# Two transformer blocks on one Trainium2 core: reordering block two's query and key chunks, moving v's range to other banks, and one selection product for the compressed blocks

## The chip, the cores and the metric

One core of one Trainium2 chip runs the whole program in one launch. The metric is device time in microseconds for one execution, the median of several. The engines are named as the profile names them: PE is TensorE (matrix products, with PEld its weight loads), DVE is VectorE, ACT is ScalarE, POOL is GpSimd, and SP is SyncE, which here only issues transfers. Each engine runs its own instruction list in order and waits for the others on semaphores.

## The reference, cut to what is computed

Two blocks are applied one after the other to a sequence of 256 tokens of width 1024. The change lies in the second block, in the projection and the attention that follow its first norm:

```python
p = _split_columns(u @ w_in)          # q_a k_a v_a | q_b k_b v_b | q_idx k_idx w_idx | q_c k_cmp v_cmp k_sel v_sel k_win v_win g_c | g_merge
o_a = _stick_breaking(heads(q_a), heads(k_a), heads(v_a))
o_b = _dsa_attention(_rope(q_b), rope1(k_b), v_b, _rope(q_idx), rope1(k_idx), w_idx)
o_c = _nsa_attention(_rope(q_c), rope1(k_cmp), v_cmp, rope1(k_sel), v_sel, rope1(k_win), v_win, gates, ...)
g = sigmoid(g_merge)
merged = g0 * (o_a @ w_up[0]) + g1 * (o_b @ w_up[1]) + g2 * (o_c @ w_up[2])

def _compress(tok, pos_emb, w1, w2):  # inside _nsa_attention, for k_cmp and v_cmp: 15 blocks of 32 tokens
    blocks = tok[:, idx] + pos_emb
    hid = gelu(blocks.reshape(B, n_cmp, 32 * 64) @ w1)   # 128 wide
    return hid @ w2
```

The queries are 4 heads of 64, so each of q_b, q_idx and q_c is 256 columns of the projection; k_b, k_idx, k_sel, k_win, k_cmp and v_cmp are 64 columns each. All inputs and outputs are 32-bit floats.

## The kernel before

**Products in parts.** A large product is computed from split operands. A weight slot arrives by DMA (`low`), ACT rounds it into a high part (`split` in `scalar_program`, by halves of its eight row tiles), DVE subtracts to get the low part (`split` in `vector_program`, L2705), and PE multiplies high by high, low by high and high by low. The high parts stand in two buffers that alternate, so the split of slot j+1 can begin when slot j-1 has been multiplied.

**Block two's projection, `main_b`.** After the two chunks of the `head` (q_a and k_a, in `plan_2[0]` and `plan_2[1]`), a stream `st2` of slots j = 0, 1, 2 ... is worked off. Slots 0 to 4 are the feature chunks `plan_2[2]` to `plan_2[6]`, each of which leaves its columns on the partitions: q_b, q_idx, q_c (256 columns each), then one chunk of four 64-column pieces (k_b, k_idx, k_sel, k_win), then one of 128 columns (k_cmp, v_cmp). Slots 5 and 6 are the two halves of v's range (464 columns, tokens on the partitions, `token_range`), slots 7 to 18 the six gate ranges. A chunk of 256 columns is two halves of 24 products on PE (L794, L795 alternating, then eight of L803); the chunk of 128 columns is one such half. Nothing else runs beside `main_b`; every engine goes through its list alone.

**What each engine does for chunk j, in order.** ACT: split both halves of slot j+1, wait for chunk j's last product, read its bank (`rope_read`: one copy and four swapped copies), go on. A hand-written exception, `ahead`, takes the first half of slot 5 before the read of chunk 3. After the last chunk's read ACT waits for the rotation of the key chunk and makes three copies of keys to the other half of the partitions (`key_act`, L2377 to L2382). DVE: subtract both halves of slot j+1, then rotate chunk j-1 (`rope2`: cosine, sine, add at L2806, L2808, L2810). PE: the banks of PSUM alternate 0, 1 by `pg` for the chunks, and v's range takes the next two of the same cycle, 1 and 0; a bank is taken over only after its reader is done. With v's first row range read, DVE copies two more keys (`key_dve`).

**Slots and transfers.** SP issues the loads in one list: `st2` slots go in turn to memory slots 3, 0 and 5, a load waiting for the chunk that held its slot. Behind slots 0 and 1 it issues the four halves of the compression weights (`cmp_w1`, 2 MB) and four small ones (`cmp_w2`), then slot 2 and so on. A chunk of 256 adjacent columns is one transfer with rows of 1024 bytes; the chunk of four pieces is four transfers with rows of 256 bytes.

**After `main_b`.** `turns.drive` interleaves the six gate ranges (main) with `nsa_keys`, `dsa(1)`, `dsa(0)`, `stick` and then `nsa(0)`, `nsa(1)` (sides), one step each in turn, in the same order on every engine. `nsa_keys` sums 32 products per row group into banks 5 and 6 (four row groups of 32 rows, because `w1` is applied to the 16 columns of `blk` by four different row positions), DVE copies them to `hd`, and a product with four pieces of the identity (L1607, eight products with 16 columns) transposes them and adds the four groups up in bank 7; then DVE and ACT apply the gelu. POOL builds `blk` from the rotated k_cmp and v_cmp. Constants (`C_...`) come with one transfer of 2 MB early in the program, issued by ACT.

Of the kernel before, what the change touches and what calls it, by code (L numbers as in the profile page):

```python
# [29 lines left out]
C_COS = C_CMM + 30  # L30
# [3 lines left out]
C_END = C_SINC + 256  # L34
# [10 lines left out]
def shape_constants():  # L45
# [37 lines left out]
    c[0:64, C_SINC:C_SINC + 256] = np.concatenate([-sin, sin])  # L83
    return c
# [189 lines left out]
def program(nc, A, consts, vecs, pt, out):  # L274
    with ExitStack() as ctx:
# [150 lines left out]
        def rope_to(n):  # L426


            return RC[:, 6:10:3, :] if n == 5 else RC[:, 10:11, :] if n == 6 else RC[:, 2 * (n - 2):2 * (n - 2) + 2, :]
# [45 lines left out]
        def rslot3(n, nk, width):  # L475
# [7 lines left out]
        plan_2 = [([(0, 256, 0)], [128, 128]), ([(256, 256, 0)], [128, 128]), ([(768, 256, 0)], [128, 128]),  # L483
                  ([(1152, 256, 0)], [128, 128]), ([(1476, 256, 0)], [128, 128]),
                  ([(1024, 64, 0), (1408, 64, 64), (1860, 64, 128), (1988, 64, 192)], [128, 128]), ([(1732, 128, 0)], [128])]
# [217 lines left out]
        def tensor_program(e, turns):  # L703
# [131 lines left out]
            def token_range(st, j0, n, w, freed, late):  # L835
                nk = 8 // n
                banks = [next(pg), next(pg)]
# [700 lines left out]
            def scores(done, name, i, qc, kc_, W, freed):  # L1538
# [3 lines left out]
                q.wait_ge(*rope_dve.at("in2", 5))  # L1542
# [44 lines left out]
            def nsa_keys():  # L1587
# [31 lines left out]
            def nsa(i):  # L1619
# [7 lines left out]
                q.wait_ge(*rope_dve.at("in2", 4))  # L1627
# [167 lines left out]
        def scalar_program(e, turns):  # L1795
# [78 lines left out]
            def ahead(st, j):  # L1874

                return st.tag == "st2" and j == 5

            def feature_chunk(st, j, widths, read):
                steps = 1 + len(widths)
                for n in range(steps):  # L1880
                    if n == 1 or n == 0 and not ahead(st, j + 1):
                        split(st, j + 1, (n,))
                    yield
                q.wait_ge(*main_pe.at(st.tag, j, 1))
                if ahead(st, j + 2):
                    split(st, j + 2, (0,))
                read()
                yield

            def token_range(st, j0, n, read):  # L1890
                nk = 8 // n
                banks = [next(pg), next(pg)]
                for s in range(n):
                    for i in range(2):
                        for r in range(nk // 2):
                            if i == 0 and (r == 1 or r == 0 and not ahead(st, j0 + s + 1)):
                                split(st, j0 + s + 1, (r,))
                            yield
# [461 lines left out]
            def read2(n, b):  # L2360
                if n < 2:
                    copy(QA[:, 2 * n:2 * n + 2, :], halves(bank(b))).then_inc(main_act.up("qa", n), 1)
                else:
                    m = 1 if n == 6 else 2
# [8 lines left out]
            def main_b():  # L2373
                for n in range(2, 7):
                    b = next(pg)
                    yield from feature_chunk(st2, n - 2, plan_2[n][1], lambda: read2(n, b))
                    if n == 6:  # L2377
                        q.wait_ge(*rope_dve.at("in2", 5))
# [4 lines left out]
                yield from token_range(st2, 5, 2, read_vt)  # L2383
# [232 lines left out]
        def vector_program(e, turns):  # L2616
# [127 lines left out]
            def token_range(st, j0, n, read, late):  # L2744
                nk = 8 // n
                banks = [next(pg), next(pg)]
# [543 lines left out]
            def rope2(n):  # L3290
                if n >= 2:
                    m = 1 if n == 6 else 2
                    rope("in2", n, m, rz2[n % 2][:, 0:m, :], rope_to(n), *((C_COSC, C_SINC) if n == 6 else (C_COS, C_SIN)))

            def read_vt(i, p):
                if i == 0:
                    q.wait_ge(*rope_dve.at("in2", 5))
# [9 lines left out]
            def main_b():  # L3307
# [3 lines left out]
                yield from token_range(st2, 5, 2, read_vt, lambda: rope2(6))  # L3311
# [341 lines left out]
        def gpsimd_program(e, turns):  # L3653
# [177 lines left out]
            def nsa_keys():  # L3831
# [3 lines left out]
                q.wait_ge(*rope_dve.at("in2", 6))  # L3835
# [126 lines left out]
```

## Time and profile before

| | us |
|---|---|
| median of 3 runs (lowest, highest) | 909.61 (909.11, 909.75) |
| the profiled execution, device time | 909.91 |
| its span, first to last instruction | 907.4 |
| busy PE / DVE / ACT / POOL | 882.2 / 606.8 / 480.5 / 29.2 |
| granted clock of TensorE, mean | 0.998 |

The profile gives the span of the first to the last instruction; the device time of the same execution is 2.5 us longer. Times in the rows below are from the start of the span. `main_b` fills 493.1 to 533.5 us, the gate ranges and their sides follow up to about 661 us. A timeline row gives the start, the duration, engine, line, what is written from what, and in brackets how long the engine had been idle and what ended that. Matmul ends are modelled and overlap the next start, so that distances on PE are taken from start to start.

### The profile page before, as it was taken

The page shows a single profiled execution, that of the slowest core. Times are in us where ns is not written, and L with a number is a line of the kernel's source. Part 1 is how long each engine was busy: PE and PEld are TensorE (multiplying, and loading weights), DVE is VectorE, ACT ScalarE, POOL GpSimd, SP SyncE. Part 2 cuts the span into 40 slices and gives each one's busy share as a digit, 9 for nine tenths or more (in the row PEclk, how much of TensorE's full clock was granted, in tenths as well). Part 3 has the DMA queues.
Part 4 walks back from the last instruction along what each step waited for, and adds up shares of the span by engine and source line. Part 5 has one row for each costly group of instructions (what it writes and reads, how often), then busy time and mean ns, then how long its engine had stood idle before and what let it go on. Part 6 is the DMA issues. An engine that isn't in the chain of part 4 may idle for free.

```text
span 907.4 us, 15435 instructions
## 1 busy us (share of the span) xinstructions
PE 882.2 (97%) x6552; PEld 748.8 (83%) x6552; DVE 606.8 (67%) x976; ACT 480.5 (53%) x775; POOL 29.2 (3%) x51
## 2 busy tenths in 40 slices
PE   7999999999899999999999999999999999999997
PEld 4999898787689888888889978776788788888885
DVE  4578978557856666656766577877863566666673
ACT  4775667436534444456444856484622545555561
POOL 0010000010000000000000020000000000000000
PEclk9999999999999999999999999999999999999999
DMA  9644333224468665555339764353817566665521
GB/s 336 190 140 140 99 119 114 63 83 150 178 248 282 188 190 190 200 202 187 121 112 229 164 210 144 111 186 107 277 38 206 146 187 188 191 193 194 199 95 47
DMA packets 131204, 150.71 MB, mean 166 GB/s; under 512 B 11808, under 2 KB 102176, under 8 KB 131008
## 3 DMA queue, kind: packets, MB, share of 16 engines
q1 hardware_dynamic: 129920, 145.57, 51.8%
q10 hardware_dynamic: 1216, 4.16, 1.2%
q8 instruction: 52, 0.85, 0.4%
q14 instruction: 16, 0.13, 0.0%
HBM read 148.67 MB, written 1.05 MB: 165 GB/s over the span
## 4 chain that ended last, share of the span: by engine, by line
PE 85%; DVE 7%; ACT 4%; issue 2%; DMA 1%; POOL 0%; POOLq 0%; ACTq 0%; DVEq 0%
PE psum L821 12%; PE psum L716 9%; PE psum L718 9%; PE psum L717 9%; PE psum L826 7%; PE psum L774 4%; PE psum L794 3%; PE psum L795 3%; PE psum L803 3%; PE psum L722 3%; PE psum L870 2%; PE psum L880 2%; PE psum L871 2%; PE psum L827 2%; DVE parts L2705 2%
## 5 line engine op out<-in xcount | busy, mean ns | idle before, releaser
L1808 ACT ACTIVATE parts<-low 128x1024 fp32r<-128x1024 f32 (+3 forms) x252 | 254.3, 1044 | 65.6 <-PE psum L718 48.3
L2705 DVE TENSOR_TENSOR parts<-low,parts 128x1024 fp32r<-128x1024 f32 (+3 forms) x156 | 183.7, 1206 | 37.7 <-ACT parts L1808 37.5
L716 PE MATMUL psum<-parts 128*128 128x512 f32 (+2 forms) x424 | 169.1, 399 | 4.6 <-DVE parts L2705 2.5
L718 PE MATMUL psum<-parts 128*128 128x512 f32 (+2 forms) x424 | 163.5, 386 | 0.0
L717 PE MATMUL psum<-parts 128*128 128x512 f32 (+2 forms) x424 | 163.4, 385 | 0.0
L1808 ACT ACTIVATE high<-psum 128x512 f32<-128x512 f32 (+6 forms) x115 | 63.4, 560 | 134.2 <-PE psum L827 76.4
L821 PE MATMUL psum<-parts 128*128 128x512 f32 x462 | 116.8, 392 | 0.0
L716 PEld LDWEIGHTS psum<-parts 128*128 128x128 f32 x424 | 79.6, 188 | 26.3 <-DVE parts L2705 4.5
L821 PEld LDWEIGHTS psum<-parts 128*128 128x128 f32 x462 | 86.9, 188 | 16.9
L718 PEld LDWEIGHTS psum<-parts 128*128 128x128 f32 x424 | 79.6, 188 | 16.4
L717 PEld LDWEIGHTS psum<-parts 128*128 128x128 f32 x424 | 79.8, 188 | 13.9
L2770 DVE TENSOR_TENSOR parts<-low,parts 128x1024 fp32r<-128x1024 f32 x54 | 66.0, 1222 | 35.3 <-ACT parts L1808 35.3
L794 PE MATMUL psum<-parts 128*128 128x256 f32 (+2 forms) x312 | 79.0, 291 | 0.0
L795 PE MATMUL psum<-parts 128*128 128x256 f32 (+2 forms) x312 | 76.5, 282 | 0.0
L826 PEld LDWEIGHTS psum<-parts 128*128 128x128 f32 x528 | 72.0, 190 | 5.1
L826 PE MATMUL psum<-parts 128*128 128x256 f32 x528 | 73.6, 282 | 0.0
L794 PEld LDWEIGHTS psum<-parts 128*128 128x128 f32 (+2 forms) x312 | 58.9, 189 | 2.2 <-issue 1.2
L795 PEld LDWEIGHTS psum<-parts 128*128 128x128 f32 (+2 forms) x312 | 59.0, 189 | 0.3 <-issue 0.3
L3197 DVE TENSOR_TENSOR mid<-psum,high 128x512 f32<-128x512 f32 x33 | 22.8, 692 | 46.2 <-ACT high L1808 46.2
L1808 ACT ACTIVATE mid<-psum 32x512 f32<-32x512 f32 (+7 forms) x61 | 32.9, 552 | 31.5 <-PE psum L803 12.9
L803 PE MATMUL psum<-parts 128*128 128x256 f32 (+2 forms) x312 | 43.8, 283 | 0.0
L803 PEld LDWEIGHTS psum<-parts 128*128 128x128 f32 (+2 forms) x312 | 40.1, 189 | 0.0
(313 smaller groups left out, 1310.6 us busy)
## 6 DMA issues: line engine op xcount, KB each, us to landing
low<-in_w_in_dram SPq DMA_DIRECT2D x40, 1024.0 KB, 5.3
low<-in_w_ffn_in_dram SPq DMA_DIRECT2D x44, 512.0 KB, 5.2
low<-in_w_ff_in_dram SPq DMA_DIRECT2D x16, 1024.0 KB, 5.7
low<-in_w_ff_out_dram SPq DMA_DIRECT2D x16, 1024.0 KB, 4.8
low<-in_w_ffn_out_dram SPq DMA_DIRECT2D x11, 1024.0 KB, 5.0
low<-in_w_out_dram SPq DMA_DIRECT2D x8, 1024.0 KB, 5.2
low<-in_w_ple_gate_dram SPq DMA_DIRECT2D x4, 1024.0 KB, 5.0
low<-consts_dram ACTq DMA_DIRECT2D x1, 2078.0 KB, 9.0
```

Of the source, the lines that this page charges most:

```text
L716: mm(o, l[0], r[0], start, False)
L717: mm(o, l[0], r[1], False, False)
L718: return mm(o, l[1], r[0], False, stop)
L774: t = mm(PSUM[0:m, banks[n], 256 * j + 128 * i:256 * j + 128 * i + 128], w3[:, k, off:off + m], uT[:, k, 128 * i:128 * i + 128], k == 0, k ...
L794: mm(o, hi[:, k, c], st.uh[:, k, :], k == 0, False)
L795: mm(o, lo_[:, k, c], st.uh[:, k, :], False, False)
L803: t = mm(o, hi[:, k, c], st.ul[:, k, :], False, k == 7)
L821: mm(p, hi[:, k, c], st.u2(k), k == 0, False)
L826: mm(p[:, 0:256], lo_[:, k, c], st.uh[:, k, :], False, False)
L1808: return e.activation(o, a, ACT.Copy)
L2705: tt(rslot3(n, nk, width)[:, r, 0:w], slot3(n, nk, width)[:, r, 0:w], st.hi3(j)[:, r, 0:w].bitcast(F32), ALU.subtract) \
L2770: tt(rview(OR + 2048 * n + 1024 * (k % 2), 1024), slot(n)[:, 1024 * (k % 2):1024 * (k % 2) + 1024], rview(base, 1024).bitcast(F32), ALU.su ...
```

## The change

- `plan_2` is reordered: the four-piece key chunk first (n = 2, slot 0), the 128-column chunk of k_cmp and v_cmp second (n = 3, slot 1), then q_b, q_idx and q_c (n = 4, 5, 6, slots 2 to 4). `rope_to`, the widths and the constants follow the new numbers, and so do the waits for keys (now for n = 2, and for n = 3 on POOL); the waits for queries are all for the last rotation, n = 6.
- ACT's key copies come behind the read of chunk n = 4 and no longer at the end.
- ACT's exception `ahead` is gone: every slot is split in two halves in the regular places.
- v's range is given banks 5 and 6 on all engines.
- The eight products with pieces of the identity become two with a new constant `C_SEL` (16 of its 128 columns are used; row r selects column r % 32), which makes the constants' transfer 64 KB longer and moves what lies behind them in memory.

```diff
-C_END = C_SINC + 256
+C_SEL = C_SINC + 256
+C_END = C_SEL + 128
...
+    c[:, C_SEL:C_SEL + 16] = r % 32 == s[:, 0:16]
...
-            return RC[:, 6:10:3, :] if n == 5 else RC[:, 10:11, :] if n == 6 else RC[:, 2 * (n - 2):2 * (n - 2) + 2, :]
+            return RC[:, 6:10:3, :] if n == 2 else RC[:, 10:11, :] if n == 3 else RC[:, 2 * (n - 4):2 * (n - 4) + 2, :]
...
-        plan_2 = [([(0, 256, 0)], [128, 128]), ([(256, 256, 0)], [128, 128]), ([(768, 256, 0)], [128, 128]),
-                  ([(1152, 256, 0)], [128, 128]), ([(1476, 256, 0)], [128, 128]),
-                  ([(1024, 64, 0), (1408, 64, 64), (1860, 64, 128), (1988, 64, 192)], [128, 128]), ([(1732, 128, 0)], [128])]
+        plan_2 = [([(0, 256, 0)], [128, 128]), ([(256, 256, 0)], [128, 128]),
+                  ([(1024, 64, 0), (1408, 64, 64), (1860, 64, 128), (1988, 64, 192)], [128, 128]), ([(1732, 128, 0)], [128]),
+                  ([(768, 256, 0)], [128, 128]), ([(1152, 256, 0)], [128, 128]), ([(1476, 256, 0)], [128, 128])]
...
-            def token_range(st, j0, n, w, freed, late):
+            def token_range(st, j0, n, w, freed, late, banks=None):
                 nk = 8 // n
-                banks = [next(pg), next(pg)]
+                banks = banks or [next(pg), next(pg)]
...
-                yield from token_range(st2, 5, 2, 464, lambda i: [main_act.at("vt2", i), main_dve.at("vt2", i)], nothing)
+                yield from token_range(st2, 5, 2, 464, lambda i: [main_act.at("vt2", i), main_dve.at("vt2", i)], nothing, (5, 6))
...
-                q.wait_ge(*rope_dve.at("in2", 5))
+                q.wait_ge(*rope_dve.at("in2", 6))
...
-                    for g in range(4):
-                        t = mm(p[:, 16 * h:16 * h + 16], hd[:, h, :], ident[:, 32 * g:32 * g + 16], g == 0, g == 3)
+                    t = mm(p[:, 16 * h:16 * h + 16], hd[:, h, :], const(C_SEL, 16), True, True)
...
-            def ahead(st, j):
-
-                return st.tag == "st2" and j == 5
-
             def feature_chunk(st, j, widths, read):
                 steps = 1 + len(widths)
                 for n in range(steps):
-                    if n == 1 or n == 0 and not ahead(st, j + 1):
+                    if n < 2:
                         split(st, j + 1, (n,))
                     yield
                 q.wait_ge(*main_pe.at(st.tag, j, 1))
-                if ahead(st, j + 2):
-                    split(st, j + 2, (0,))
                 read()
                 yield
...
-                    if n == 6:
-                        q.wait_ge(*rope_dve.at("in2", 5))
+                    if n == 4:
+                        q.wait_ge(*rope_dve.at("in2", 2))
                         for m, half in enumerate(half_rows[::-1]):
                             copy(RC[half, 7, :], RC[half_rows[1], 6, :]).then_inc(key_act.up(m), 1)
...
-                q.wait_ge(*rope_dve.at("in2", 6))
+                q.wait_ge(*rope_dve.at("in2", 3))
```

## Rows read from the trace of the kernel before

**Rows 1.** Waits of PE, 490 to 660 us: total, times, longest.

```profile
PE psum L716 <- DVE parts L2705: 2.5, 3, 1.5
PE psum L716 <- ACT high L1808: 1.2, 1, 1.2
...
PE psum L1632 <- DVE high L3377: 0.4, 2, 0.3
```

**Rows 2.** Timeline of PE in the projection: chunk starts, a last half, v's range, gates.

```profile
498.95 0.28 PE L794 MATMUL psum<-parts 128*128 128x256 f32 x1
...
504.71 0.30 PE L794 MATMUL psum<-parts 128*128 128x256 f32 x1
...
518.30 1.12 PE L803 MATMUL psum<-parts 128*128 128x256 f32 x8
520.66 0.48 PE L716 MATMUL psum<-parts 128*128 128x464 f32 x1 [1.24 <-ACT high L1808]
...
522.82 0.48 PE L716 MATMUL psum<-parts 128*128 128x464 f32 x1 [0.63 <-DVE parts L2705]
...
528.37 0.48 PE L716 MATMUL psum<-parts 128*128 128x464 f32 x1 [1.49 <-DVE parts L2705]
...
533.53 0.40 PE L716 MATMUL psum<-parts 128*128 128x512 f32 x1
```

**Rows 3.** Timeline of ACT in the projection: read, split, read of 128 columns, key copies.

```profile
499.15 3.02 ACT L1808 ACTIVATE high<-psum 128x512 f32<-128x512 f32 x5 [3.27 <-PE psum L803]
502.20 2.01 ACT L1808 ACTIVATE parts<-low 128x1024 fp32r<-128x1024 f32 x2
...
521.63 1.95 ACT L1808 ACTIVATE high<-psum 128x256 f32<-128x256 f32 x5
524.73 1.30 ACT L1808 ACTIVATE high<-high 64x256 f32<-64x256 f32 x3 [1.14 <-DVE high L2810]
```

**Rows 4.** Timeline of DVE in the projection: subtractions and a rotation.

```profile
503.29 2.36 DVE L2705 TENSOR_TENSOR parts<-low,parts 128x1024 fp32r<-128x1024 f32 x2 [5.96 <-ACT parts L1808]
505.57 0.69 DVE L2806 TENSOR_TENSOR high<-high,low 128x512 f32<-128x512 f32 x1
```

**Rows 5.** SP's timeline (issues), then transfers issued 494 to 495 and 492 to 512: KB each, us to landing.

```profile
477.76 0.99 SPq L610 DMA_DIRECT2D low<-in_w_in_dram  x2
...
494.17 0.43 SPq L610 DMA_DIRECT2D low<-in_w_in_dram  x1
...
low<-in_w_in_dram SPq DMA_DIRECT2D x1, 1024.0 KB, 7.1
low<-in_w_in_dram SPq DMA_DIRECT2D x4, 256.0 KB, 4.1
```

**Rows 6.** Stretches, all engines: last columns are granted clock, DMA share, GB/s.

```profile
480.00:482.00 2.00, 2.00 (x20) 2.00 (x19) 1.33 (x3) 0.41 (x1) 0.55 (x1) 1.00 1.08 379
...
486.00:488.00 2.00, 2.00 (x18) 2.00 (x19) 0.88 (x3) 1.02 (x1) 0.00 (x0) 1.00 1.21 195
...
503.00:504.00 1.00, 1.00 (x11) 1.00 (x10) 0.71 (x1) 1.00 (x2) 0.00 (x0) 1.00 1.24 274
```

**Rows 7.** Timeline of PE: the identity products, and the next idle stretch behind them.

```profile
557.79 1.72 PE L1607 MATMUL psum<-low,mid 128*128 128x16 f32 x14
559.35 0.49 PE L716 MATMUL psum<-parts 128*128 128x512 f32 x1
...
567.74 0.50 PE L716 MATMUL psum<-parts 128*128 128x512 f32 x1 [0.41 <-DVE parts L2705]
```

**Rows 8.** Timelines of ACT and DVE: where each last waited before 567.74.

```profile
551.05 0.60 ACT L1804 ACTIVATE high<-psum 128x512 f32<-128x512 f32 x1 [2.14 <-PE psum L718]
...
560.56 1.76 DVE L2629 SCALAR_TENSOR_TENSOR high<-high 128x1536 f32<-128x1536 f32 x1 [2.40 <-ACT high L1804]
```

**Rows 9.** Stretches at the program's end: PE busy stands second, granted clock third from last.

```profile
901.00:902.00 1.00, 0.40 (x2) 0.00 (x0) 0.56 (x1) 0.00 (x0) 0.00 (x0) 1.00 0.00 0
...
904.00:905.00 1.00, 0.00 (x0) 0.00 (x0) 0.30 (x1) 0.46 (x1) 0.00 (x0) 0.56 0.00 0
```

More of the change, by code:

```diff
@@ L1626, in nsa @@
                     bank(b)
-                q.wait_ge(*rope_dve.at("in2", 4))
+                q.wait_ge(*rope_dve.at("in2", 6))
                 q.wait_ge(*cmp_act.at("kc"))
@@ L1884, in feature_chunk, with token_range @@
                 q.wait_ge(*main_pe.at(st.tag, j, 1))
-                if ahead(st, j + 2):
-                    split(st, j + 2, (0,))
                 read()
                 yield
-            def token_range(st, j0, n, read):
+            def token_range(st, j0, n, read, banks=None):
                 nk = 8 // n
-                banks = [next(pg), next(pg)]
+                banks = banks or [next(pg), next(pg)]
                 for s in range(n):
@@ L1895, in token_range @@
                         for r in range(nk // 2):
-                            if i == 0 and (r == 1 or r == 0 and not ahead(st, j0 + s + 1)):
+                            if i == 0 and r < 2:
                                 split(st, j0 + s + 1, (r,))
@@ L2363, in read2 @@
                 else:
-                    m = 1 if n == 6 else 2
+                    m = 1 if n == 3 else 2
                     rope_read("in2", n, m, b, rz2[n % 2][:, 0:m, :], rope_to(n))
@@ L2382, in main_b @@
                         copy(RC[half_rows[1], 6, :], RC[half_rows[0], 6, :]).then_inc(key_act.up(2), 1)
-                yield from token_range(st2, 5, 2, read_vt)
+                yield from token_range(st2, 5, 2, read_vt, (5, 6))
             turns.alone(main_b())
@@ L2742, in feature_chunk, with token_range @@
                 yield
-            def token_range(st, j0, n, read, late):
+            def token_range(st, j0, n, read, late, banks=None):
                 nk = 8 // n
-                banks = [next(pg), next(pg)]
+                banks = banks or [next(pg), next(pg)]
                 for s in range(n):
@@ L3291, in rope2 @@
                 if n >= 2:
-                    m = 1 if n == 6 else 2
-                    rope("in2", n, m, rz2[n % 2][:, 0:m, :], rope_to(n), *((C_COSC, C_SINC) if n == 6 else (C_COS, C_SIN)))
+                    m = 1 if n == 3 else 2
+                    rope("in2", n, m, rz2[n % 2][:, 0:m, :], rope_to(n), *((C_COSC, C_SINC) if n == 3 else (C_COS, C_SIN)))
             def read_vt(i, p):
                 if i == 0:
-                    q.wait_ge(*rope_dve.at("in2", 5))
+                    q.wait_ge(*rope_dve.at("in2", 2))
                     for m, half in enumerate(half_rows):
@@ L3310, in main_b @@
                     yield from feature_chunk(st2, n - 2, plan_2[n][1], lambda: rope2(n - 1), nothing)
-                yield from token_range(st2, 5, 2, read_vt, lambda: rope2(6))
+                yield from token_range(st2, 5, 2, read_vt, lambda: rope2(6), (5, 6))
             turns.alone(main_b())
```

## The prediction

> **What bounds the kernel now.** The table comes first: PE is busy 882.2 of 907.4 us, so what can be won is where PE stands still. Second, the list of waits for 490 to 660 us, the part the change touches. PE waits there 2.5 us in three pieces for DVE's subtraction and 1.2 us for ACT's reading of a bank, then 0.4 us for DVE in the attention [rows 1]. Third, PE's timeline shows that the first two lie in v's range. The short chunk's last eight products start at 518.30 and take 8 x 0.12 us (a 256-column chunk is 48 of them, 504.71 - 498.95 = 5.76 us), so v could start at 519.26. It starts at 520.66, stops again until 522.82 and until 528.37, and the gates begin at 533.53 [rows 2]. The last 24 products of v need 533.53 - 528.37 = 5.16 us, so 48 need about 10.2 of the 14.27 us between 519.26 and 533.53: **4.05 us are lost there**, the ceiling of what the reordering can win. With 0.15 us that the earlier chunks lose, I set the loss of `main_b` before to 4.2 us.
>
> The reason is in the timelines of ACT and DVE. Per 256-column chunk ACT reads the bank in 3.02 us and splits the next slot in 2.0 us [rows 3], and DVE's first subtraction follows 1.09 us behind the start of the first split and takes 1.18 us [rows 4]. From a chunk's end at 498.95 this chain ends at 499.15 + 3.05 + 1.09 + 1.18 = 504.47, and PE needs it at 504.71 [rows 2 to 4]: 0.24 us of slack in a 5.76 us period. A chunk of half that length, 2.88 us, must therefore stop PE for about 2.6 us, wherever it stands. Before, it stands last, ACT has that stop eased by `ahead`, and the bank wait and key copies fall into the same place.
>
> **The change, part by part.** I carry the absolute times of the trace on, with slot 0 (now the keys) ending at 498.95 as before.
>
> *A, the short chunk second, `ahead` gone.* PE does chunk 1 in 2.88 us, until 501.83. ACT reads the keys from 499.15 to 502.20, then splits slot 2; DVE has the first half at 504.47, and a wait costs 0.06 us more (520.66 and the other starts lie that far behind their releases): PE goes on at 504.53, **2.70 us late**. The second half comes at 499.15 + 3.05 + 1.09 + 2.36 = 505.65 [rows 3, 4], due at 505.49, another 0.2 us. A = 2.9 us; chunk 2 ends at 510.5.
>
> *A', slot 2's load.* SP issues slots 0 and 1 from 477.76, then the compression weights, and slot 2 at 494.17, which lands 7.1 us later, at 501.3 [rows 5]; ACT wants it at 502.20, so 0.9 us are spare. Now slot 0 is four transfers with rows of 256 bytes. The trace moves such rows at 274 GB/s where they are not held up by their issue, and 1024-byte rows at 379 GB/s; the 512-byte rows of the weights go at 195 GB/s [rows 6]. So 1.05 MB take 3.8 us and not 2.8, and slot 1, half the bytes in 512-byte rows, takes 0.52 MB / 195 = 2.7 us as against 2.8. The queue has work without a pause until slot 2, so that lands about 0.9 us later, at 502.2; three more issues stand before it, each about half a microsecond (0.99 us for two, [rows 5]), of which I count a third as not covered by transfers under way: 502.8. I take 0.6 us on PE's path. Bounds: nothing (the transfers under way cover all) and 2.2 us (256-byte rows at the slowest rate shown, 195 GB/s: 5.4 us and not 2.8, less the spare of 0.9, and the same 0.5 us of issues).
>
> The Trainium skill, DMA: Bandwidth & Descriptors, section "Why small descriptors are slow (HBM only)", puts a 256-byte row at 8 of 11 bus cycles. That would be about 0.73 of full rate, an estimate from that page, against 274/379 = 0.72 in rows 6: the trace agrees, and the sum is the same by either.
>
> *B, the key copies.* They move from the end, where they delay slot 6's split, to between the read of chunk 2 and slot 4's split: 1.3 us [rows 3] in a chain with 0.24 us of slack. Slot 3's halves are ready early (ACT is free from about 508), so chunk 3 follows without a stop, to 516.3. ACT: 510.5 + 0.2 + 3.05 + 1.3 = 515.1; DVE's first half 515.1 + 1.09 + 1.18 = 517.3. Chunk 4 starts **1.1 us late**, with 0.2 more at its second half. B = 1.3; chunk 4 ends at 523.4.
>
> *C, v's range.* With banks 5 and 6 the wait for bank 1 (1.2 us, [rows 1]) is gone, and slot 5's halves are split by 522.2 and subtracted by 523.3, so v starts at once and its first slot runs to about 528.5. Slot 6 is split after the read of chunk 4, 523.6 + 3.05 = 526.65 and on to 527.65, but on DVE it stands behind the last rotation, whose second step waits for that read: two steps of about 0.65 us (0.69 each in [rows 4], overlapped), then the subtraction, 1.1 us: 529.1. C = 0.7 us; bounds 0.4 (the rotation's steps overlap more) and 1.3 (all three behind the read).
>
> *Gate slots.* Slot 7 loads when chunk 4 ends, 3 to 4 us later than before, and PE wants it 11 us after that; a transfer of this size takes 5 to 7 us [rows 5]. Nothing. The longer constants are loaded in the first 25 us and wanted at the fourth chunk: 64 KB at 379 GB/s is 0.2 us of queue, nothing on PE. POOL's additions start some 15 us earlier and nobody waited for them (they are not in [rows 1]): nothing. The scores' later key, n = 6, is rotated about 6 us before the gates begin: nothing. With the loads of slots 5 and 6 it is the same, since they start by chunk 2 and 3 as before.
>
> *D, the selection product.* L1607's eight products are 16 instructions, 14 of them in 559.35 - 557.79 = 1.56 us, so 0.11 us each [rows 7]; two products are four, and **1.3 us** fall away on PE. But the next thing PE waits for is DVE's subtraction at 567.74, with 0.41 us idle already [rows 7]. DVE works without a pause from 560.56, where it was released by ACT's logarithm, and ACT's own last wait was for PE at 551.05 [rows 8], before the products. So PE reaches 567.74 earlier and waits there 1.7 us. D = 0; bounds -1.3 (won after all) and 0.
>
> **Sum.** A 2.9 + A' 0.6 + B 1.3 + C 0.7 + D 0 = 5.5 us lost, against 4.2 before: **+1.3 us**. PE has as many stops as it had, so their restarts cancel. The profiled execution took 909.91 us (its span 907.4 and 2.5 around it, which the change leaves alone) and would take 911.2; the median of the runs shown is 0.3 us below it, so the forecast by the median is 909.61 + 1.3 = 910.9.
>
> **The rivals.**
>
> *R1, slower by the late load.* The place is ACT's split of slot 2 at 502.20. Every microsecond that the slot lands after it is a microsecond of PE, and nothing behind takes it back, since `main_b` has no slack. It decides from a landing at 503.3 on, where the sum passes +1.8. For it: four issues more in front, and a stretch in which SP was held up by a full queue (a single load took 7.1 us, [rows 5]). Against: 0.9 us spare. With the upper bound of A' the time is 910.9 + 1.6 = 912.5. A longer stop might also lower the clock: at the end PE stops in 901 to 902 and the granted clock has fallen to 0.56 of full speed (a mean between the two levels, 2.4 and 1.2 GHz) in 904 to 905 [rows 9]. No stop inside the program shows it; half a chunk at half speed would take 2.9 us more, 913.8 with the sum as it stands. The Trainium skill, TensorE: Matmul & The Clock Gate, section "What's actually happening", says the same, that an idle array falls to half clock; no run here shows it within a stage.
>
> *R2, faster.* A stop of 2.9 us lets ACT and DVE get ahead, the slack this makes carries B and C, and D is won because DVE's chain ends earlier as well: 2.9 + 0 - 4.2 - 1.3 = -2.6, 907.3. Against: ACT's reads and splits each wait for PE's last product of a chunk, so the lead is gone one chunk later, and D is anchored at 551.05.
>
> *R3, D is won, the rest as in the sum*: 910.9 - 1.3 = 909.6, no difference. Against it [rows 8].
>
> **How the numbers follow.** 0.2% of 909.6 us, about what a measurement of this kernel can tell from no change, is 1.8 us: faster is below 907.8, slower above 911.4. The forecast (sum between +0.2 and +1.8) has 0.47, R3 0.09, other mixtures within the bound 0.01; R1 0.30, of which a tenth with the lowered clock; R2 0.13. So faster 0.13, same 0.57, slower 0.30. The range leaves out R2 and the lowered clock: from the sum with A' 0, B 0.9, C 0.4 and D won (4.2 - 4.2 - 1.3, so 908.3) to the upper bounds of A' and C (1.6 and 0.6 more, 913.1).
>
> **What would show it.** In the changed profile: PE idle about 2.7 us ahead of chunk 2 (near 504.5) and 1.1 us ahead of chunk 4 (near 517.4), both released by DVE L2705; v's first product without a wait, one stop of 0.4 to 1.3 us in its middle; gates near 534.6 and not 533.5; L1607 with four instructions and the idle time at the next L716 grown to 1.7 us. Wrong would be: a landing of slot 2 behind 503.3 (R1), gates at or before 533.5 (R2), no growth of that idle time (R3).

## The result and the profile after

The changed kernel takes **913.51 us** (median of 5 runs, 913.31 to 914.45) against 909.75 for the kernel before (909.11 to 909.94): ratio 1.0045, interval [1.0033, 1.0056]. It is slower by 3.8 us where 1.3 us and "no difference" were forecast, and it lies above the range. The profiled execution of the changed kernel took 913.51 us, its span is 911.6 us against 907.4. One execution each of x_load and x_banks below took over 2239 us, and their medians leave it out. Lines stand a little lower or higher in the changed file (L716 to L718 are L718 to L720, L2705 is L2700, L1808 is L1809, L1597, the compression product, is L1599).

The waits of PE between 490 and 660 us (total, times, longest) answer to [rows 1]:

```profile
PE psum L796 <- ACT high L1809: 2.7, 1, 2.7
PE psum L1599 <- issue: 1.4, 1, 1.4
PE psum L718 <- DVE parts L2700: 1.4, 2, 0.8
PE psum L796 <- DVE parts L2700: 1.1, 1, 1.1
...
PE psum L718 <- ACT high L1805: 0.4, 1, 0.4
```

Four of the five are the steps A, B, C and D of the prediction. The list names ACT for the first of them (A). PE waits there for two things: the reading of its bank, which ACT had ended at 502.13, and DVE's subtraction of the first half (the first of the two below, done at 504.52). PE started 0.15 us behind the subtraction, as it did at 519.00, where DVE is named (0.14); so it was DVE, as forecast:

```profile
503.30 2.36 DVE L2700 TENSOR_TENSOR parts<-low,parts 128x1024 fp32r<-128x1024 f32 x2 [7.50 <-ACT parts L1809]
```

The second line of the list has no releaser ("issue" is time in which PE waited for nothing that the profile shows) and stands in no step. PE's timeline puts each in its place, as [rows 2] and [rows 7] did:

```profile
504.67 0.36 PE L796 MATMUL psum<-parts 128*128 128x256 f32 x1 [2.72 <-ACT high L1809]
...
505.32 0.41 PE L796 MATMUL psum<-parts 128*128 128x256 f32 x1
505.54 0.41 PE L797 MATMUL psum<-parts 128*128 128x256 f32 x1
...
519.00 0.35 PE L796 MATMUL psum<-parts 128*128 128x256 f32 x1 [1.10 <-DVE parts L2700]
...
530.71 0.48 PE L718 MATMUL psum<-parts 128*128 128x464 f32 x1 [0.55 <-DVE parts L2700]
...
535.88 0.40 PE L718 MATMUL psum<-parts 128*128 128x512 f32 x1
...
547.00 2.00 PE L1599 MATMUL psum<-high,mid 64*32 64x128 f32 x124
550.42 0.41 PE L1599 MATMUL psum<-high,mid 64*32 64x128 f32 x4 [1.42 <-issue]
550.76 0.50 PE L718 MATMUL psum<-parts 128*128 128x512 f32 x1
...
568.99 0.48 PE L718 MATMUL psum<-parts 128*128 128x512 f32 x1 [0.40 <-ACT high L1805]
571.88 0.50 PE L718 MATMUL psum<-parts 128*128 128x512 f32 x1 [0.81 <-DVE parts L2700]
```

The reader should see two things that the list of waits can't show or doesn't name. First, behind the stop at 504.67 the products stand 0.21 us apart (505.32, 505.54) and not 0.12. They are busy, so no wait tells of it. The stretches of the changed kernel do (PE busy stands second, the granted clock third from last):

```profile
504.00:505.00 1.00, 0.33 (x3) 0.36 (x4) 1.00 (x2) 0.95 (x3) 0.00 (x0) 1.00 1.07 351
505.00:506.00 1.00, 1.00 (x8) 1.00 (x7) 1.00 (x2) 0.96 (x4) 0.00 (x0) 0.54 1.11 365
506.00:507.00 1.00, 1.00 (x6) 1.00 (x6) 0.96 (x3) 0.98 (x2) 0.00 (x0) 0.50 0.88 272
507.00:508.00 1.00, 1.00 (x7) 1.00 (x6) 1.00 (x2) 1.00 (x2) 0.00 (x0) 0.50 0.08 28
508.00:509.00 1.00, 1.00 (x9) 1.00 (x8) 1.00 (x2) 0.20 (x1) 0.00 (x0) 0.76 0.00 0
509.00:510.00 1.00, 1.00 (x11) 1.00 (x10) 1.00 (x2) 0.00 (x0) 0.00 (x0) 1.00 0.00 0
```

The granted clock is 0.50, the 1.2 GHz level, for some 3.5 us. Second, the compression product breaks off four instructions before its end, for 1.42 us.

To compare executions I count from the start of the second chunk, which is 498.95 before [rows 2] and 498.91 in the changed kernel:

| us from the second chunk's start | before | after | difference |
|---|---|---|---|
| gates begin | 34.58 | 36.97 | +2.4 |
| compression product begins | 45.70 | 48.09 | +2.4 |
| first gate product behind it | 47.66 | 51.85 | +4.2 |
| end of the span | 408.45 | 412.69 | +4.2 |

So 2.4 us are lost before the gates and 1.8 in the compression product; nothing behind it takes any back.

### The profile page after: what moved, and what is told of

It reads as the page before. It is cut to its first block, busy times and chain, and to the rows that moved or that the text cites. A ratio compares the mean times of both kernels' runs of the same rounds, so it can differ in the third digit from the quotient of the medians.

```text
span 911.6 us, 15411 instructions
## 1 busy us (share of the span) xinstructions
PE 883.3 (97%) x6540; PEld 749.4 (82%) x6540; DVE 606.3 (67%) x976; ACT 480.4 (53%) x775; POOL 26.1 (3%) x51
## 4 chain that ended last, share of the span: by engine, by line
PE 82%; DVE 7%; ACT 4%; issue 2%; DMA 2%; SPq 2%; POOL 0%; POOLq 0%; ACTq 0%; DVEq 0%
PE psum L823 12%; PE psum L718 9%; PE psum L720 9%; PE psum L719 9%; PE psum L828 7%; PE psum L796 3%; PE psum L797 3%; PE psum L724 3%; PE psum L805 3%; PE psum L872 2%; PE psum L882 2%; PE psum L873 2%; PE psum L776 2%; PE psum L829 2%; DVE parts L2700 2%
## 5 line engine op out<-in xcount | busy, mean ns | idle before, releaser
L1809 ACT ACTIVATE parts<-low 128x1024 fp32r<-128x1024 f32 (+2 forms) x252 | 254.2, 1044 | 63.8 <-PE psum L720 48.3
L2700 DVE TENSOR_TENSOR parts<-low,parts 128x1024 fp32r<-128x1024 f32 (+3 forms) x156 | 183.4, 1205 | 41.2 <-ACT parts L1809 41.0
L718 PE MATMUL psum<-parts 128*128 128x512 f32 (+2 forms) x424 | 168.9, 398 | 2.6 <-DVE parts L2700 1.4
L720 PE MATMUL psum<-parts 128*128 128x512 f32 (+2 forms) x424 | 163.6, 386 | 0.0
L1809 ACT ACTIVATE high<-psum 128x512 f32<-128x512 f32 (+6 forms) x115 | 63.3, 559 | 139.1 <-PE psum L829 76.4
L718 PEld LDWEIGHTS psum<-parts 128*128 128x128 f32 x424 | 79.6, 188 | 23.9 <-issue 3.8
L720 PEld LDWEIGHTS psum<-parts 128*128 128x128 f32 x424 | 79.6, 188 | 16.3
L796 PE MATMUL psum<-parts 128*128 128x256 f32 (+2 forms) x312 | 80.2, 294 | 3.8 <-ACT high L1809 2.7
L797 PE MATMUL psum<-parts 128*128 128x256 f32 (+2 forms) x312 | 77.6, 285 | 0.0
L1809 ACT ACTIVATE mid<-psum 32x512 f32<-32x512 f32 (+7 forms) x61 | 32.8, 552 | 31.3 <-PE psum L805 13.0
L805 PE MATMUL psum<-parts 128*128 128x256 f32 (+2 forms) x312 | 44.0, 284 | 0.0
```

The source lines that it names most:

```text
L718: mm(o, l[0], r[0], start, False)
L720: return mm(o, l[1], r[0], False, stop)
L796: mm(o, hi[:, k, c], st.uh[:, k, :], k == 0, False)
L797: mm(o, lo_[:, k, c], st.uh[:, k, :], False, False)
L805: t = mm(o, hi[:, k, c], st.ul[:, k, :], False, k == 7)
L1809: return e.activation(o, a, ACT.Copy)
```

## The experiments

The ratios are to the kernel before, timed beside each kernel on the same chip; its median there lay between 909.28 and 909.63 us. A difference of medians that were not taken beside each other, such as one to the 913.51 us of the changed kernel, can be off by as much as the kernel before moves (909.28 to 909.75).

| kernel | median us | ratio, interval |
|---|---|---|
| x_fill | 910.49 | 1.0011 [1.0001, 1.0021] |
| x_load | 912.39 | 1.0034 [1.0023, 1.0045] |
| x_fill_load | 911.93 | 1.0028 [1.0018, 1.0037] |
| x_keys | 912.34 | 1.0030 [1.0017, 1.0044] |
| x_land | 913.6 | 1.0048 [1.0034, 1.0062] |
| x_stick | 911.81 | 1.0023 [1.0013, 1.0033] |
| x_pad | 911.78 | 1.0022 [1.0013, 1.0032] |
| x_banks | 911.59 | 1.0023 [1.0013, 1.0033] |
| x_prod | 909.41 | 1.0001 [0.9992, 1.0010] |
| x_wait | 909.61 | 1.0003 [0.9993, 1.0013] |
| v_first | 909.48 | 1.0004 [0.9995, 1.0013] |
| v_best | 907.47 | 0.9979 [0.9971, 0.9988] |
| v_best2 | 906.2 | 0.9965 [0.9951, 0.9978] |

The first seven are the changed kernel with an edit, the rest the kernel before with one.

### The stop and the clock

**x_fill** adds twenty products to PE ahead of chunk 2, into a bank that nothing reads.

```diff
                 for n in range(2, 7):
+                    if n == 4:
+                        p = bank(7)
+                        for _ in range(20):
+                            mm(p[:, 0:256], st2.uh[:, 0, 0:128], st2.uh[:, 0, :], True, True)
                     yield from feature_chunk(st2, n - 2, next(pg), plan_2[n][1], read2(n), nothing)
```

> The changed kernel with 20 products of its own normed input, written to the unused bank 7, put ahead of chunk 2: they fill the 2.9 us in which PE stood still there, and their result is not read. Theory (the stop lowers the clock): the granted clock stays at 1.00 through 504 to 509, the first half of chunk 2 takes 3.0 us and not 4.4, and the time falls by 1.5 us, to 912.0 (ratio to before 1.0026). Rival (the slow products of chunk 2 come from something else that runs then, the transfers or DVE): still 0.21 us a product, 913.5 (1.0045).

PE's timeline of x_fill, and below it a stretch behind the stop (columns as above):

```profile
501.05 2.56 PE L1457 MATMUL psum<-parts 128*128 128x256 f32 x20
503.88 0.35 PE L796 MATMUL psum<-parts 128*128 128x256 f32 x1 [0.27 <-ACT high L1813]
...
533.71 0.40 PE L718 MATMUL psum<-parts 128*128 128x512 f32 x1
...
544.83 2.03 PE L1603 MATMUL psum<-high,mid 64*32 64x128 f32 x128
```

```profile
504.00:506.00 2.00, 2.00 (x17) 1.94 (x18) 2.00 (x3) 1.94 (x5) 0.00 (x0) 1.00 0.97 333
```

PE works through the stop, ACT's chain ends at the same point of the chunk (5.7 us behind its start), and the clock stays at 1.00. The second chunk starts at 498.17 here, so the gates begin 35.54 us behind it, 0.96 later than before, where the changed kernel is 2.39 later: the lowered clock costs **1.4 us**. The pause in the product is gone too (x128 in one row), which I had not meant to change; x_pad below says why. With both gone the change costs 1.1 us by the medians.

**x_fill_load** is x_fill with the load of slot 10 held back as in x_load (next part).

> Both edits at once (20 filling products ahead of chunk 2, slot 10 loaded behind the compression product). Theory: both losses go, 913.5 - 1.5 - 1.8 = 910.2 (1.0007), so what is left of the change is the sum of its stops, +0.7 us. Rival (one loss, two symptoms): the gain is that of one of the two alone, 911.8 to 912.0.

The clock stays at 1.00 and there is no pause, as in x_fill, but the median is 1.4 us above x_fill's and 1.7 above what was expected. The profiled execution is the lowest of nine and shows only one new wait, for work that comes from slot 10, so most of that is not accounted for:

```profile
563.06 0.67 PE L1509 MATMUL psum<-high,low 128*128 128x256 f32 x2 [0.33 <-DVE high L2630]
```

**x_keys** moves ACT's key copies behind chunk 4's split, to the first reading of v's bank.

```diff
             def read_vt(i, p):
+                if i == 0:
+                    q.wait_ge(*rope_dve.at("in2", 2))
+                    for m, half in enumerate(half_rows[::-1]):
...
-                    if n == 4:
-                        q.wait_ge(*rope_dve.at("in2", 2))
-                        for m, half in enumerate(half_rows[::-1]):
...
```

> The changed kernel with ACT's three key copies put ahead of its reading of v, where ACT is idle, and no longer between the read of chunk 2 and the split of slot 4. Theory: the stop of 1.26 us ahead of chunk 4 goes, all else stays: 912.3 (1.0030). Rival (the stop comes from the late chunk 2, not from the copies): it stays, 913.5 (1.0045).

The stop of 1.10 us ahead of chunk 4 is gone and the median is 1.2 us lower: B was the copies, and its 1.1 us lay on PE's path. The stop ahead of chunk 2 (2.67 us), the lowered clock behind it and the pause (1.51 us) are all still there.

**x_land** issues the compression weights behind slot 2 and not ahead of it, so that slot 2 can land earlier.

```diff
-                if j == 1:
+                if j == 2:
                     q.wait_ge(*wo_pe.at("pg", "y", 1, 1))
```

> The changed kernel with the compression weights issued behind slot 2 and no longer ahead of it, so that slot 2 lands some 10 us before ACT wants it. Theory: the stop ahead of chunk 2 is 2.9 us in every run, since ACT's reading sets it; the clock still falls, the pause in the compression product stays: 913.4 (1.0045) as in the profile of the changed kernel. Rival (the landing of slot 2 sets the stop in most executions): 1 us less or more, 912.4 (1.0033), and a smaller spread.

The same stop (2.67 us), the same lowered clock, the same time: the landing doesn't set the stop in a usual execution. That it can was seen once, in the profiled execution of x_load, on ACT (and PE's stop was 4.11 us there, not 2.7):

```profile
503.31 1.06 ACT L1811 ACTIVATE parts<-low 128x1024 fp32r<-128x1024 f32 x1 [1.47 <-DMA low<-in_w_in_dram]
```

### The pause in the compression product

PE's program is itself fetched by a DMA queue ("instruction"), 16 KB at a time. (That queue q8 is PE's is argued from its size, 51 blocks and 0.84 MB in the changed kernel, where PE has 13,080 of the 14,882 instructions on the page, and from the runs below.) Around the product the views of the transfers show one such block: in the kernel before, from 541.5 to 542.0 us, alone; in the changed kernel, from 548.0 to 548.5, behind the data of slot 10's load, which SP issued at 543.70.

```profile
q8 instruction: 1, 0.02, 16.8%
```

```profile
543.70 0.37 SPq L612 DMA_DIRECT2D low<-in_w_in_dram  x1
...
q1 hardware_dynamic: 36, 0.05, 27.5%
q8 instruction: 1, 0.02, 12.2%
```

**x_banks** is the kernel before with v's range in banks 5 and 6 on all engines, and nothing else of the change.

```diff
-                banks = [next(pg), next(pg)]
+                banks = banks or [next(pg), next(pg)]
...
-                yield from token_range(st2, 5, 2, 464, lambda i: [main_act.at("vt2", i), main_dve.at("vt2", i)], nothing)
+                yield from token_range(st2, 5, 2, 464, lambda i: [main_act.at("vt2", i), main_dve.at("vt2", i)], nothing, (5, 6))
```

> The kernel before with v's range in banks 5 and 6 and nothing else. Theory: the wait of 1.2 us for bank 1 goes, but PE then waits for slot 5's second half, which ACT splits only behind the read of chunk 3; v's range ends when it did, 909.4 (1.0000). Rival (the bank wait is worth what the list of waits shows): 908.2 (0.9987).

PE's timeline of x_banks:

```profile
523.03 0.48 PE L716 MATMUL psum<-parts 128*128 128x464 f32 x1 [2.13 <-DVE parts L2705]
...
528.58 0.48 PE L716 MATMUL psum<-parts 128*128 128x464 f32 x1 [1.49 <-DVE parts L2705]
...
544.86 2.00 PE L1597 MATMUL psum<-high,mid 64*32 64x128 f32 x124
548.26 0.41 PE L1597 MATMUL psum<-high,mid 64*32 64x128 f32 x4 [1.41 <-issue]
```

The wait for the bank is gone, but with the chunks in their old order DVE takes its place (2.13 us in one stop where there were 1.24 and 0.63), so v is no faster. And the pause is there: it comes with the banks. From the product's start to the next gate product it is 3.74 us (544.86 to 548.60) against 1.96 before (544.65 to 546.61), so the pause makes 1.8 us of the 2.2 by which this kernel is slower. The gates begin 0.5 us late in this profile, for a wait of 0.36 us for DVE at 504.90, ahead of v.

**x_load** is the changed kernel, with slot 10's load held back until PE has done the product (issued at 550.33, while the block comes at 546.3).

```diff
             for j, (pieces, _) in enumerate(st.slots):
+                if j == 10:
+                    q.wait_ge(*cmp_pe.at("w1", 3, 1))
                 load(("st2", j), (3, 0, 5)[j % 3], [cols(*p) for p in pieces], main_pe.at("st2", j, 1))
```

> The changed kernel with the load of slot 10 issued only when the compression product (L1599) is done, so that no transfer of data runs beside that product. Theory (a block of PE's code is fetched behind the data of slot 10): PE's pause of 1.4 us inside the product is gone, 911.8 (1.0022). Rival (the pause lies in where the block ends in PE's list, whatever else is moved): the pause stays, 913.5 (1.0045). ACT wants slot 10 only about 5 us after that point, so the later load itself costs nothing or a few tenths.

The pause is gone, but the median is only 1.1 us below the changed kernel's. The profiled execution has the late slot 2 shown above, and a wait of 0.4 us for DVE like that of x_fill_load: a load that goes out 6.6 us later brings a wait of its own.

**x_stick** holds the same load back by 2 us only.

```diff
+                if j == 10:
+                    q.wait_ge(*stick_pe.at("s", 2))
```

> The changed kernel, with one thing more: SP holds back the load of slot 10 until PE is through the second sticky product, some 1.6 us later than it goes out now (ACT asks for slot 10 some 8 us after that). Theory (the pause inside the compression product is the fetch of PE's next code block, which stands in the DMA engines behind the data of slot 10's load): the block arrives ahead of the load's data, the pause of 1.4 us is gone, and the time is 913.5 - 1.8 = 911.7, ratio to the kernel before 1.0025; the lowered clock behind chunk 1 stays, as nothing ahead of it is changed. Rival (the pause belongs to the place in PE's list, whatever the load does): 913.5, ratio 1.0045, the pause still there.

911.81 where 911.7 was expected. The pause is gone (PE's timeline of x_stick), the block comes at 546.0, the load's data behind 546.5; the stop ahead of chunk 2 and the lowered clock are unchanged.

```profile
547.16 2.03 PE L1601 MATMUL psum<-high,mid 64*32 64x128 f32 x128
549.12 0.50 PE L720 MATMUL psum<-parts 128*128 128x512 f32 x1
```

So the pause is the code block standing behind the load's data. From the product's start to the next gate product it is 1.96 us here, as before, and 3.76 in the changed kernel, so the pause costs 1.8 us; the medians differ by 1.7. What made the block late was still open.

**x_wait** adds one entry to PE's list in the kernel before: a wait for a value already waited for.

```diff
+                q.e.wait_ge(main_act.handle, q.past[main_act])
                 yield from token_range(st2, 5, 2, 464, lambda i: [main_act.at("vt2", i), main_dve.at("vt2", i)], nothing)
```

> The kernel before with one instruction more on PE and nothing else: ahead of v's range PE waits once more for a value that it has already waited for, so the wait itself holds nothing up. PE's list up to the compression product is then as long as in the changed kernel, which has one wait more there. Theory (the length of PE's list sets when its next code block is fetched, and one entry more moves the fetch from just ahead of slot 10's load to behind its data): a pause of about 1.4 us inside the compression product, the code block's bytes behind the load's, and 909.5 + 2.0 = 911.5, ratio to the kernel before 1.0022, as with banks 5 and 6 alone. Rival (the pause comes with the banks or with the later time of the product): no pause, 909.5, ratio 1.0000.

No pause, no difference: the theory that one entry more is enough fell. It had overlooked where the waits stand. With v in banks 0 and 1, the four waits for those banks (two engines, two banks) stand ahead of the gates' slots that use them next. With v in banks 5 and 6 they stand directly ahead of the compression product, which is the next user of banks 5 and 6, and by the code the gate and side products before it come some three entries earlier in the list.

**x_pad** gives that back: the changed kernel with four idle waits ahead of v.

```diff
+                for _ in range(4):
+                    q.e.wait_ge(main_act.handle, q.past[main_act])
                 yield from token_range(st2, 5, 2, 464, lambda i: [main_act.at("vt2", i), main_dve.at("vt2", i)], nothing, (5, 6))
```

> The changed kernel with four more entries in PE's list and nothing else: ahead of v's range PE waits four times for a value that it has already waited for. In the changed kernel four waits, for the two banks that v leaves, stand directly ahead of the compression product; in the kernel before they stand ahead of the gates' slots, so that every entry between lies some three places further on in PE's list. Theory (PE asks for its next code block at a fixed place of its list, and with the waits behind the gates' work that place is reached later, behind the start of slot 10's load): four entries ahead of v put the gates' work back to its old place, the block comes ahead of the load's data, no pause, 913.5 - 1.8 = 911.7, ratio to the kernel before 1.0025. Rival (it isn't the place in the list; the waits that stand directly ahead of the product hold the fetch up, wherever the list stands): the pause of 1.4 us is still there, 913.5, ratio 1.0045.

911.78 where 911.7 was expected. PE's timeline of x_pad, and the transfers of 542.5 to 543.0 us:

```profile
499.31 0.28 PE L796 MATMUL psum<-parts 128*128 128x256 f32 x1
...
505.01 0.36 PE L796 MATMUL psum<-parts 128*128 128x256 f32 x1 [2.67 <-ACT high L1811]
...
534.85 0.40 PE L718 MATMUL psum<-parts 128*128 128x512 f32 x1
...
545.97 2.03 PE L1601 MATMUL psum<-high,mid 64*32 64x128 f32 x128
547.93 0.50 PE L718 MATMUL psum<-parts 128*128 128x512 f32 x1
```

```profile
q8 instruction: 1, 0.02, 16.3%
```

The block is there about 3.1 us ahead of the product again, as in the kernel before (3.0), x_prod (3.2) and x_fill (3.1, whose twenty products lengthen the list as well). Where the list is not lengthened and the load is out of the way, it comes 1.1 to 1.8 us ahead (x_stick, x_load, v_best, v_best2). Waits that hold nothing up thus moved the fetch by over a microsecond, past the start of a load. The load's data run beside the product here too (383 GB/s from 546 to 547 us) and PE doesn't pause, so it is not the data as such that stops it. No run shows which entry of the list asks for a block.

This execution shows a second thing: behind a stop of 2.67 us its clock did **not** fall (stretches, columns as above).

```profile
505.00:506.00 1.00, 0.99 (x8) 0.99 (x8) 1.00 (x2) 0.98 (x3) 0.00 (x0) 1.00 1.07 367
506.00:507.00 1.00, 1.00 (x10) 0.95 (x9) 1.00 (x2) 0.96 (x3) 0.00 (x0) 1.00 1.09 352
```

The stretches of x_pad show it, and its gates begin 35.54 us behind the second chunk, as in x_fill. In the five other profiles with this stop (2.66 to 2.72 us in the changed kernel, x_keys, x_land and x_stick, 4.11 in x_load) the clock fell. The lowered clock is thus a risk that such a stop runs, and not a fixed price. Of x_pad's ten times three lie between 910.09 and 910.70 and seven between 911.36 and 912.48, as they would with and without it, but only the profiled execution (910.70) has its clock shown here.

A shorter stop runs the risk too. All fifteen profiles have a stop of 1.44 to 1.84 us near 231 us, in a part of the program that no edit touches (1.75 in the kernel before). Fourteen kept the full clock behind it; v_best2's, the slowest of its five executions, did not (a row of PE's timeline, then a stretch):

```profile
231.42 0.50 PE L1397 MATMUL psum<-parts 128*128 128x512 f32 x1 [1.76 <-ACT mid L1806]
...
233.00:234.00 1.00, 1.00 (x4) 0.76 (x3) 1.00 (x2) 0.75 (x2) 0.00 (x0) 0.50 1.04 387
```

The stop of 2.13 us in x_banks was not followed by a lower clock.

### The selection product

**x_prod** is the kernel before with the selection product and its constant, and nothing else.

```diff
-                    for g in range(4):
-                        t = mm(p[:, 16 * h:16 * h + 16], hd[:, h, :], ident[:, 32 * g:32 * g + 16], g == 0, g == 3)
+                    t = mm(p[:, 16 * h:16 * h + 16], hd[:, h, :], const(C_SEL, 16), True, True)
```

> The kernel before with the eight identity products made two by the selection constant and nothing else. Theory: 1.3 us less work on PE, and as much more waiting for DVE ahead of the next products, 909.4 (1.0000). Rival (the work was on the path that sets the end): 908.1 (0.9986).

909.41 against 909.39. PE's timeline of x_prod:

```profile
564.30 0.47 PE L718 MATMUL psum<-parts 128*128 128x512 f32 x1 [0.40 <-ACT high L1805]
567.19 0.50 PE L718 MATMUL psum<-parts 128*128 128x512 f32 x1 [0.83 <-DVE parts L2706]
```

PE is idle for 0.40 + 0.83 us here and 0.41 before [rows 7]. From the first gate product behind the compression product to the one at 567.19 (567.74 before) it is 21.13 us in both kernels: what the products gave up is waited for.

### What would have won

**v_first** keeps the old order of the chunks, takes banks 5 and 6, and puts ACT's splits of slots 5 and 6 ahead of the reads they stood behind, and DVE's subtraction of slot 6 ahead of the last rotation.

```diff
                 q.wait_ge(*main_pe.at(st.tag, j, 1))
-                if ahead(st, j + 2):
-                    split(st, j + 2, (0,))
+                if st.tag == "st2" and j >= 3:
+                    split(st, j + 2)
                 read()
...
-                yield from token_range(st2, 5, 2, read_vt, lambda: rope2(6))
+                yield from token_range(st2, 5, 2, read_vt, lambda: (split(st2, 6), rope2(6)), (5, 6))
```

> The kernel before with its own order of chunks, v's range in banks 5 and 6, and on ACT the splits of slots 5 and 6 taken before the reads of chunks 3 and 4 (DVE subtracts slot 6 before it rotates the last chunk). Theory (what stops PE around the short chunk is the order of ACT's reads and splits, together with the bank): all three stops of v's range go, 4.0 us less than before, 905.4 (ratio 0.9956). Rival (the reads pushed back hold PE up in turn, by the banks or by DVE's rotation): no gain, 909.4 (1.0000).

v's three stops are gone, and the time is that of before. PE's timeline of v_first:

```profile
531.20 0.47 PE L716 MATMUL psum<-parts 128*128 128x512 f32 x1 [0.16 <-DVE parts L2701]
...
533.78 0.50 PE L716 MATMUL psum<-parts 128*128 128x512 f32 x1 [0.95 <-DVE parts L2701]
...
543.67 2.00 PE L1597 MATMUL psum<-high,mid 64*32 64x128 f32 x124
547.50 0.41 PE L1597 MATMUL psum<-high,mid 64*32 64x128 f32 x4 [1.84 <-issue]
```

Its second chunk starts at 500.26: the gates begin 3.6 us earlier than before, the product 2.3, and the first product behind the pause (547.84) 0.1. In this execution, the slowest of eleven, the clock fell behind the pause of 1.84 us as well:

```profile
549.00:550.00 1.00, 1.00 (x4) 0.81 (x3) 0.97 (x5) 0.00 (x0) 0.00 (x0) 0.50 0.00 0
```

**v_best** is v_first with slot 10's load held back as in x_stick.

> The kernel before with v's range in banks 5 and 6, ACT's splits of slots 5 and 6 and DVE's split of slot 6 put ahead of the reads and rotations that stood before them (the run v_first), and slot 10's load held back by the second sticky product. Theory: v_first won v's three stops, 4 us, and gave them back to the pause in the compression product and the lowered clock behind it; without the pause both stay away and the time is 909.5 - 4.0 = 905.5, ratio to the kernel before 0.9957. Rival (what v_first won is lost again in a later wait, the later load or DVE in the attention): 909.4, ratio 1.000.

907.47 where 905.5 was expected. The theory was right on the pause and too high on the gain: of v's 4 us, 1.1 had gone to DVE's subtraction of slot 7 at the gates, as the rows of v_first show, and I had not taken it off. In v_best's profile the gates begin 3.5 us earlier than before and the product 2.2; the median is 2.05 lower.

**v_best2** is v_best with that subtraction ahead of DVE's reading of v's bank.

```diff
+                            if (st.tag, j0 + s + 1) == ("st2", 7):
+                                if (i, r) == (0, 1):
+                                    split(st, 7)
-                            if (i, r) in ((0, 1), (1, 0)) and (st.tag, j0 + s + 1) != ("st2", 6):
+                            elif (i, r) in ((0, 1), (1, 0)) and (st.tag, j0 + s + 1) != ("st2", 6):
```

> v_best, with DVE subtracting both halves of slot 7 before it copies v's bank out. Theory (the gates' stops of 0.95 and 0.16 us in v_first are DVE's subtraction of slot 7 standing behind that copy): 1.0 us less than v_best, 904.5, ratio to the kernel before 0.9946. Rival (the copy is then late and the next user of its bank waits instead): the same as v_best, 905.5.

906.2 (five executions, 905.43 to 907.93), which is 1.3 us below v_best, 3.3 below the kernel before and 7.3 below the changed kernel, the fastest median of all.

## Why the prediction was wrong

**A** was right: due at 501.79, chunk 2 started at 504.67, 2.88 us late for 2.70 forecast, with 2.72 of idle time for about 2.7. In x_pad, at full clock, the step costs 3.0 us in all for 2.9. **A'** was next to nothing and not 0.6 in the profile: slot 2, issued at 494.59, landed 7.6 us later, at 502.2, just as ACT's read ended, and ACT's split follows that read directly (499.11 + 3.02, then 502.21). x_land gained nothing by an earlier landing. The 0.9 us that were spare were thus used up, as forecast, and the 0.6 us beyond them did not come, though x_load's execution shows that the landing can decide.

```profile
499.11 3.02 ACT L1809 ACTIVATE high<-psum 128x512 f32<-128x512 f32 x5 [4.12 <-PE psum L805]
502.21 2.00 ACT L1809 ACTIVATE parts<-low 128x1024 fp32r<-128x1024 f32 x2
```

**B** was right (1.10 of idle time for 1.1; x_keys), **C** nearly (0.55 for 0.7, with no wait at v's start), and **D** was right: 0, with the idle time in two places, 0.40 and 0.81 us, and not 1.7 in one. The sum of these steps was right too: +1.3 was forecast, or +0.7 without A', and the executions with neither lowered clock nor pause lose 0.96 us up to the gates (x_fill, x_pad). That it comes so near to +1.3 is partly luck, as A' fell away while A and B each cost 0.1 to 0.2 us more than forecast (3.0 and 1.5 in x_pad). (A slip of the prediction's: R2's 907.3 counts from the profiled execution, and by the median it is 907.0.)

**The first step that failed** is the price of the lowered clock. The prediction saw that a longer stop might lower it, but tied it to the late load and gave it a tenth of R1's 0.30. It came behind the on-time stop of A, which the forecast itself contained. The size was off too: 2.9 us were named and 1.4 found, because the half clock lasted 3.5 us and not the 5.8 of a half chunk. The stop that the change makes is longer than any in the kernel before once PE has begun (2.7 against 1.75 near 231 us and 1.49 in v's range [rows 2]), and the prediction gave the fall of the clock at the program's end [rows 9] too little weight for it. R1, slower, was thus right in sign and wrong in mechanism.

The Trainium skill, TensorE: Matmul & The Clock Gate, section "What's actually happening", was quoted there for the half clock of an idle array. The profile of the changed kernel agrees, with 0.50 behind 2.72 us; x_pad's shows that 2.67 us can also pass without it, and v_best2's has it behind 1.76.

**The second is a term that was missing.** The banks of v were costed by the wait that they remove. That the waits for them move too, and with them the place in PE's list at which a code block is fetched, stood nowhere; nor did the load of slot 10, on whose data the block then waits. It cost 1.8 us in the profile (4.2 less 2.4), 1.7 by the medians of x_stick and x_pad. The profile before showed what it takes: the block at 541.5, and the load issued 541.35. The block was ahead of the load's data by less than a microsecond, and the prediction read no transfers there.

Together: 1.0 by the steps, 1.4 by the clock, 1.8 by the pause, 4.2 us of span. With the lowered clock alone the forecast would have been near 912.3, with both near 914.

What stays open: why the clock fell behind five of six stops of about 2.7 us or more and not behind the sixth, why it fell behind two shorter ones, and which entry of PE's list asks for a code block.

## What to carry to other kernels

A stop that is moved is not the same stop when it gets longer. Behind the stop of 1.4 to 1.8 us near 231 us the clock fell in one of fifteen profiles here, behind the one of about 2.7 us or more ahead of chunk 2 in five of six, for some 3.5 us each time. So price a longer stop with the chance of a lowered clock, or give PE products to work through it. When a change moves waits in an engine's list, look up when its code blocks are fetched and which bulk load is issued next to them; a pause with "issue" as its releaser is the sign. And where an engine's chain of read, split and subtract is the limit, put the next slot's split ahead of the read, as v_best2 does, rather than reorder the chunks.

## What was not expected of the hardware

- A fetch of 16 KB of PE's program took its turn behind a 1 MB load that SP had issued, and PE stood still for 1.41 to 1.84 us in the middle of a row of 128 products (the changed kernel, x_banks, x_keys, x_land, v_first).
- Four waits that were already fulfilled, added to PE's list, made the changed kernel 1.7 us faster (913.51 to 911.78; 1.6 us, each taken against the kernel before beside it).
- Twenty products that nobody reads made it 3.0 us faster (913.51 to 910.49; 2.6 us, each taken against the kernel before beside it), by keeping the clock up and by the shift in the list.
- The granted clock fell to 0.50 within the program behind five of six stops of about 2.7 us or more, and came back after some 3.5 us of full work. It fell once each behind 1.76 us (v_best2) and 1.84 us (v_first), and did not behind 2.13 us (x_banks) and 2.67 us (x_pad).
